# The RWKV core of a decoder step: off-diagonal part of the block inverse written to the other head's rows, outputs in the states' bank, sums of squares behind the betas' product, rows reordered

## The chip, the core and the metric

The kernel runs as one program on one core of one Trainium2 chip. The metric is the device time of one execution in microseconds (us). The engines are named as the profile names them: PE (TensorE), DVE (VectorE), ACT (ScalarE), POOL (GpSimd) and SP (SyncE, which issues the transfers). Every engine works through its own list of instructions in order and waits on semaphores for the others.

## The reference, cut to what matters

The reference is one inference step of a two-layer decoder over 512 prompt tokens and 8 sequences of 8 new tokens: layer 0 mixes with latent attention, layer 1 with RWKV-7 time mixing, and each layer has two SwiGLU feed-forward blocks. The change touches only the state recurrence of layer 1:

```python
def wkv_step(state, inp):
    r, w, k, v, a, b = inp
    sa = jnp.einsum('bhij,bhj->bhi', state, a)
    state = state * w[:, :, None, :] + sa[..., None] * b[:, :, None, :] + v[..., None] * k[:, :, None, :]
    return state, jnp.einsum('bhij,bhj->bhi', state, r)
...
    # in rwkv_time_mix: 16 heads of size 64, a = -kk, b = kk * sigmoid(...), w = decay
    state, y = lax.scan(wkv_step, wkv0.astype(f32), (...))
    mean = jnp.mean(y, axis=-1, keepdims=True)
    var = jnp.mean(jnp.square(y - mean), axis=-1, keepdims=True)
    y = ((y - mean) * lax.rsqrt(var + LNX_EPS)).reshape(b, l, d) * lnx_w.astype(f32) + lnx_b.astype(f32)
    y = y + bonus.reshape(b, l, d)
    out = (y * g.astype(f32)).astype(h.dtype) @ w_o
```

## The kernel before

Most of the program is large matrix products for the feed-forward blocks, the projections and the attention (lines 264 to 2360). The recurrence is a stage of its own, the functions core_pe, core_act, core_dve and core_pool: about 300 us of the span, from roughly 2200 to 2500 us.

The 16 heads are handled two at a time, one head in partitions 0 to 63 and the other in partitions 64 to 127 (HEADS). The 512 prompt tokens are cut into 8 chunks of 64 (NB = 8). Inside a chunk the recurrence becomes a few 64x64 matrices: an inverse of a unit triangular matrix is built by doubling (tiles MD, LD, L2, L4 and XA for the diagonal blocks, then OFF, NT, NR, N2T, N2R, N4R and PP for the part off the diagonal), and a short chain over chunks carries the state (function state(c): a product on PE into the states' bank 4, then a scaled copy to STC on ACT).

The loop is a pipeline of two stages, iteration(f, b). Its front half prepares unit f (unit 0 holds the 64 new tokens, units 1 to 8 are the eight pairs of heads in the prompt), its back half applies unit b = f - 1: states, outputs, their mean and variance, and the gate. So there are nine iterations and a final(8), and eight pairs of heads go through the back half. There is no scheduler: the order on each engine is the order in which these functions are written, and each hand-over is one wait on a named semaphore.

On PE nearly all products are 64x64 with 64 columns. A group is 16 of them (8 chunks, 2 heads); the trace shows two records for each. PSUM is eight banks of 128x512. A product takes its weights and data from the rows of one head and writes either the same head's rows of a bank or, with across=True, the other head's rows. The code often interleaves a group of the one sort with a group of the other, chunk by chunk, into different banks.

The names in the order in which one iteration passes them on PE:

- joint (L2594): products with the new sequences' states S0, 64x16; L2629: PP times RA into RA_PS, the finished R0 and AXT; head_sums(3) for the bonus; AXT times BTOKP (bank 2); R0 times BTOKP (the betas' product, L2545 PS<-R,BTOKP) into the states' bank.
- BT times AR0, then the tiles MD, LD and the doubling; state(1) to state(7) stand between them; gates(f) (L2580) gives the gate of unit f, three products 128x512.
- XA times OFF and back (semaphore z), interleaved with the output's products from MK1 and MB1 (bank 7, L2545); the state's part of the output QQ times STC (bank 7); keys(f+1); NR times NT and NT times NR (semaphore x), the first interleaved with MK0 times the values (bank 6).
- head_sums(5) over the output (its mean), N2R times PP, N2T times N2R, rates(f+1), then XA times RA (L2829, 64x64 with 128 columns, RA_PS in the same head's rows) interleaved with KTOKP times the values, N4R times PP, and head_sums(5) over the squares of the output.

POOL makes, per iteration, PT3 (sums_without_own), YL, the gate product RT (L3417), KKA (rated_keys), BT, K2 and KTI in that order at the turn of two iterations; KTI is what the products KTI and MD, LD at L2587 wait for. DVE adds into PP and XA, takes reciprocals in quarters (L3180, L3195) and has the running sum L3215. ACT copies banks to SBUF and loads a new function table whenever sigmoid, exp and square root follow each other.

Of the kernel before, what the change touches and what calls it, by code (L numbers as in the profile page):

```python
# [28 lines left out]
KD = D // P  # L29
# [69 lines left out]
def program(nc, a, o):  # L99
# [2430 lines left out]
    def core_pe(pe):  # L2530
# [46 lines left out]
        def gates(u):  # L2577
            for out, cols, p in places(u):
                for n, (w, x) in enumerate(((W2H, G1H), (W2H, G1L), (W2L, G1H))):
                    mm = pe.matmul(bank(2)[:, out], w[:, 1, p, :], x[:, cols], start=n == 0, stop=n == 2)  # L2580
            mm.then_inc(q["zag_g"], 1)
# [8 lines left out]
        def joint(p, states):  # L2590

            for j in states:
                for r in HEADS:
                    mm = pe.matmul(bank(0, r)[:, 2 * SQ * j:2 * SQ * (j + 1)].rearrange("p (k q) -> p k q", k=2), S0[r, j, :],  # L2594
                                   AXQ[r, :, p, j * SQ:(j + 1) * SQ], start=True, stop=True)
            return mm

        def iteration(f, b):
# [21 lines left out]
            if chain:  # L2620
# [3 lines left out]
                joint(p, range(0, 3))  # L2624
                wait("rac", b)
                wait("xa", xa_of(b, 4))
                for c in range(NB):
                    for r, out in zip(HEADS, HEADS[::-1]):
                        mm = pe.matmul(RA_PS[out, c], PP[r, c, :], RA[r, c], start=True, stop=True)  # L2629
                    if c < SB - 3:  # L2630
                        x = joint(p, (c + 3,))
                x.then_inc(q["ut"], 1)
# [7 lines left out]
            if chain:  # L2640
# [5 lines left out]
                mm.then_inc(q["gam"], 1)  # L2646
                wait("utc", b)
# [106 lines left out]
            if front:  # L2754
                gates(f)
            state(7)
# [3 lines left out]
            if prompt:  # L2760
                wait("xa", xa_of(f, 2))
            for c in range(NB):
                if prompt:
                    x = products(1, at(OFF), at(XA), (c,))
                if chain:
                    sums(7, at(vtok_b), at(mk1), c, start=True)
            if prompt:
                x.then_inc(q["z"], 1)
            for c in range(NB):
                if prompt:  # L2770
                    x = products(0, at(XA), at(OFF), (c,))
                if chain:
                    mm = sums(7, at(R0), at(mb1), c, start=False)
            if prompt:
                x.then_inc(q["z"], 1)
            if chain:
                mm.then_inc(q["y"], 1)
# [6 lines left out]
                mm.then_inc(q["ys"], 1)  # L2784
            if prompt and f + 1 < UNITS:
# [1031 lines left out]
```

## Time and profile before

| what | value |
|---|---|
| time, median of 3 runs | 2972.98 us (2968.17 to 2975.7) |
| time of the profiled execution | 2976.81 us |
| its span | 2974.6 us |
| PE busy | 2861.9 us, 96% |
| DVE busy | 2100.7 us, 71% |
| ACT busy | 1348.7 us, 45% |
| POOL busy | 698.3 us, 23% |
| chain that ended last, by engine | PE 86%, DVE 7%, ACT 3%, issue 3%, POOL 1% |

Busy time is the sum of an engine's instructions over the whole program; the chain is followed back from the last instruction and says on whom the end depended. In the 200 us slice from 2200 to 2400 us, which lies wholly in the recurrence, PE is busy 179.5 us, DVE 146.6, ACT 128.6 and POOL 107.8, at a granted TensorE clock of 0.98 of full speed. A row of a timeline has the start, the duration, the engine, the line, what is written from what, the shape and the count of merged instructions; in square brackets stands how long the engine sat idle before it and who ended that. "issue" there means that the profile shows nothing it waited for.

### The profile page before, as it was taken

The numbers are of one execution on the slowest core, as the hardware profiler recorded it, in microseconds if no ns is written. First come the engines' busy times: TensorE is split into PE (matmuls) and PEld (weight loads), VectorE is DVE, ScalarE is ACT, GpSimd is POOL, SyncE is SP. The second block draws the span as 40 slices with busy tenths as digits, with TensorE's granted clock in tenths as the row PEclk, the third lists the DMA queues.
The fourth block names the chain that finished last, engine by engine and source line by source line (L and its number), as shares of the span: only waits on it lengthen the run. The fifth ranks groups of instructions, "written<-read, shape, count | busy, mean of one in ns | idle before, by whom it ended". The sixth has DMA issues, their size and how long they took to land.

```text
span 2974.6 us, 65943 instructions
## 1 busy us (share of the span) xinstructions
PE 2861.9 (96%) x27215; PEld 2741.8 (92%) x27215; DVE 2100.7 (71%) x2719; ACT 1348.7 (45%) x2410; POOL 698.3 (23%) x537
## 2 busy tenths in 40 slices
PE   8999999989999998999999999999998997999999
PEld 8999998679999998999999999999987776999999
DVE  6977956656666664697795878775456777487875
ACT  4433434455555552443443344342456664334432
POOL 1321310320000001132131213344034553221330
PEclk9999999999999999999999999999999998999999
DMA  3223222010111121122222232221200001223222
GB/s 121 96 89 99 89 74 81 22 54 26 48 36 37 37 65 57 50 96 96 85 92 86 79 100 89 91 91 58 95 28 15 23 19 56 79 79 100 89 90 81
DMA packets 78970, 208.08 MB, mean 70 GB/s; under 512 B 25505, under 2 KB 42274, under 8 KB 63714
## 3 DMA queue, kind: packets, MB, share of 16 engines
q1 hardware_dynamic: 78690, 204.16, 20.8%
q8 instruction: 199, 3.26, 0.4%
q14 instruction: 81, 0.66, 0.1%
HBM read 198.63 MB, written 5.49 MB: 69 GB/s over the span
## 4 chain that ended last, share of the span: by engine, by line
PE 86%; DVE 7%; ACT 3%; issue 3%; POOL 1%; DMA 0%; POOLq 0%; ACTq 0%; DVEq 0%; SPq 0%
PE PS L469 26%; PE PS L285 23%; PE PS L1595 12%; PE PS L2207 5%; PE PS L642 5%; PE PS L2539 4%; PE PS L1622 1%; PE PS L1574 1%; PE PS L2545 1%; PE PS L2187 1%; DVE WL L269 1%; DVE DOWN L771 1%; DVE WL L435 1%; PE PS L1233 1%; PE PS L1214 1%
## 5 line engine op out<-in xcount | busy, mean ns | idle before, releaser
L408 POOL TENSOR_TENSOR WLF<-RAW 128x512 f32<-128x512 f32 x72 | 94.1, 1307 | 981.2 <-PE PS L285 657.3
L264 ACT ACTIVATE WH<-RAW 128x1536 fp32r<-128x1536 f32 (+3 forms) x112 | 171.4, 1530 | 323.9 <-PE PS L285 195.2
L269 DVE TENSOR_TENSOR WL<-RAW,WH 128x1536 fp32r<-128x1536 f32 (+3 forms) x113 | 217.7, 1927 | 117.8 <-ACT WH L264 117.8
L1595 PE MATMUL PS<-UKMH,CTH 128*128 128x384 f32 (+1 forms) x768 | 269.1, 350 | 0.9 <-POOL RQL L1536 0.9
L469 PE MATMUL PS<-XH,WH 128*128 128x288 f32 x864 | 255.1, 295 | 8.3 <-DVE M L510 8.3
L1671 DVE TENSOR_REDUCE SS<-SQ 128x4 f32<-128x512 f32 x256 | 173.5, 685 | 120.6 <-ACT SQ L1654 118.9
L469 PE MATMUL PS<-XH,WL 128*128 128x288 f32 x864 | 255.5, 296 | 0.0
L469 PE MATMUL PS<-XL,WH 128*128 128x288 f32 x864 | 254.8, 295 | 0.0
L1595 PE MATMUL PS<-UKMH,CTL 128*128 128x384 f32 (+1 forms) x768 | 252.7, 329 | 0.0
L1654 ACT ACTIVATE SQ<-PS 128x384 f32<-128x384 f32 (+1 forms) x384 | 172.3, 455 | 130.3 <-PE PS L1595 130.1
L285 PE MATMUL PS<-HH,WH 128*128 128x288 f32 x1056 | 225.3, 295 | 1.1 <-DVE WL L269 1.1
L285 PE MATMUL PS<-HH,WL 128*128 128x288 f32 x1056 | 226.0, 294 | 0.0
L285 PE MATMUL PS<-HL,WH 128*128 128x288 f32 x1056 | 224.4, 293 | 0.0
L285 PE MATMUL PS<-XH,WH 128*128 128x288 f32 x800 | 174.4, 300 | 18.4 <-DVE XL L308 17.0
L771 DVE TENSOR_TENSOR DOWN<-PS,HALF 128x1152 f32<-128x1152 f32 x64 | 86.7, 1355 | 147.0 <-PE PS L285 104.4
L420 ACT ACTIVATE WH<-RAW 128x1024 fp32r<-128x1024 f32 (+1 forms) x144 | 113.8, 838 | 135.3 <-PE PS L469 76.6
L285 PE MATMUL PS<-XL,WH 128*128 128x288 f32 x800 | 172.5, 298 | 0.0
L285 PE MATMUL PS<-XH,WL 128*128 128x288 f32 x800 | 172.3, 297 | 0.0
L285 PEld LDWEIGHTS PS<-HH,WH 128*128 128x128 f32 x1056 | 169.7, 187 | 2.1 <-DVE WL L269 2.0
L469 PE MATMUL PS<-XSL,WSH 128*128 128x288 f32 x576 | 171.4, 298 | 0.0
L469 PEld LDWEIGHTS PS<-XH,WH 128*128 128x128 f32 x864 | 162.5, 188 | 9.1 <-issue 9.1
L469 PE MATMUL PS<-XSH,WSH 128*128 128x288 f32 x576 | 170.7, 296 | 0.0
(704 smaller groups left out, 8959.4 us busy)
## 6 DMA issues: line engine op xcount, KB each, us to landing
RAW<-in_w SPq DMA_DIRECT2D x113, 1024.0 KB, 4.8
RAW<-in_w SPq DMA_DIRECT2D x48, 768.0 KB, 5.0
ROWS<-in_cache_c SPq DMA_DIRECT2D x128, 128.0 KB, 2.0
RAW<-in_w SPq DMA_DIRECT2D x16, 512.0 KB, 4.6
KRS<-in_cache_kr SPq DMA_DIRECT2D x128, 32.0 KB, 1.8
RAW<-in_w SPq DMA_DIRECT2D x8, 384.0 KB, 3.3
X<-in_x SPq DMA_DIRECT2D x4, 576.0 KB, 8.1
out_y<-X SPq DMA_DIRECT2D x8, 288.0 KB, 2.3
```

Source lines behind the costliest of these rows:

```text
L264: act.activation(WH[n % 2][:, 0:cols], RAW[n % 2][:, 0:cols], ACT.Copy).then_inc(rounded, 1)
L269: dve.tensor_tensor(WL[n % 2][:, 0:cols], RAW[n % 2][:, 0:cols], WH[n % 2][:, 0:cols].bitcast(F32), ALU.subtract).then_inc(item_split, 1)
L285: mm = pe.matmul(PS[:, s, 2 * t + half, 0:HT], w[s][:, c:c + P], v[:, k, half * HT:(half + 1) * HT], start=(x == 0 and p == 0), stop=(x == ...
L420: act.activation(WH[s][:, c], RAW[s][:, c], ACT.Copy).then_inc(gate_hi, 1)
L469: mm = pe.matmul(PS[:, s, b, 0:HT], w[wp](k), v[xp](k), start=not again and k == 0 and p == 0, stop=k == 3 and p == 2, skip_group_check=again)
L642: mm = pe.matmul(PS[:, s, 2 * t + half, 0:HT], w[s][:, c:c + P], v[:, k, half * HT:(half + 1) * HT], start=k == 0 and p == 0, stop=k == cn ...
L771: dve.tensor_tensor(DOWN[:].rearrange("p o (a t) -> p o a t", a=2), ps, halves(HALF[:]).unsqueeze(1).to_broadcast([P, 2, 2, HT]), ALU.mult ...
L1595: mm = pe.matmul(out[:, 0:c1 - c0], c[u][:, x], w, start=t == 0, stop=t == 5)
L1654: act.activation(SQ2[:, at:at + cols], src[:, first:first + cols], ACT.Square).then_inc(keys_sq, 1)
L1671: dve.tensor_reduce(SS[s % 2][:, p, half * 4:half * 4 + 4], SQ2[:, half * 512:half * 512 + 512].rearrange("p (h d) -> p h d", h=4), AX.X, ...
L2207: mm = pe.matmul(PS[:, s, 2 * t + half, 0:HT], w[s][:, c:c + P], v[:, k, half * HT:(half + 1) * HT], start=first and q_ == 0, stop=last an ...
L2539: mm = pe.matmul(cells(b)[out, c, :], lhs(r, c), rhs(r, c), start=True, stop=True)
```

## The change

On PE the products XA times RA (the part of R0 and AXT off the diagonal) are written to the other head's rows of RA_PS, so they can be interleaved with N2R times PP and N2T times N2R; PP times RA now goes to the same head's rows, and the products of joint stand ahead of it. The output is summed in bank 4, the states' bank, after the last state has been copied: the part from the states first, interleaved with MK0 times the values, then the parts from MK1 and MB1, interleaved with NR times NT and NT times NR. The products of XA with OFF lose their partners. gates(f) moves behind NT times NR and, for units above 0, to bank 5. The sums of squares move from the end of an iteration to behind the betas' product of the next. On ACT, DVE and POOL the rows are put in another order. No product is added or dropped.

The diff, cut to its core:

```diff
-                    mm = pe.matmul(bank(2)[:, out], w[:, 1, p, :], x[:, cols], start=n == 0, stop=n == 2)
+                    mm = pe.matmul(bank(5 if u else 2)[:, out], w[:, 1, p, :], x[:, cols], start=n == 0, stop=n == 2)
...
+        def crossed(c):
+
+            for r, out in zip(HEADS, HEADS[::-1]):
+                mm = pe.matmul(RA_PS[out, c], XA[r, c, :], RA[r, c], start=True, stop=True)
+            return mm
+
+        def queried(c):
+
+            for r in HEADS:
+                mm = pe.matmul(cells(4)[r, c, :], STC[r, c - 1, :], QQ[r, c, :], start=c == 1, stop=False, skip_group_check=True)
             return mm
...
                 for c in range(NB):
-                    for r, out in zip(HEADS, HEADS[::-1]):
-                        mm = pe.matmul(RA_PS[out, c], PP[r, c, :], RA[r, c], start=True, stop=True)
-                    if c < SB - 3:
-                        x = joint(p, (c + 3,))
-                x.then_inc(q["ut"], 1)
+                    for r in HEADS:
+                        mm = pe.matmul(RA_PS[r, c], PP[r, c, :], RA[r, c], start=True, stop=True)
                 mm.then_inc(q["r0"], 1)
...
                 mm.then_inc(q["gam"], 1)
+                if p:
+                    wait("y_norm", y_at(p, "sq_lo"))
+                    head_sums(5, YH, YL).then_inc(q["y_norm"], 1)
                 wait("utc", b)
...
+            for c in range(NB):
+                if front:
+                    x = products(6, at(MK0), at(vtok), (c,), across=prompt)
+                if chain and c:
+                    mm = queried(c)
...
+                if chain:
+                    sums(4, at(vtok_b), at(mk1), c, start=False)
...
                     x = products(1, at(NT), at(NR), (c,))
+                if chain:
+                    mm = sums(4, at(R0), at(mb1), c, start=False)
...
+            if prompt:
+                gates(f)
+                wait("pp", f)
+                wait("zc", 3 * f - 1)
+                wait("rvc", n)
+                for c in range(NB):
+                    x = products(2, at(N2R), at(PP), (c,))
+                    if c % 2:
+                        crossed(c // 2)
+                x.then_inc(q["x"], 1)
+                wait("xt", 2 * f)
+                for c in range(NB):
+                    x = products(0, at(N2T), at(N2R), (c,))
+                    if c % 2:
+                        mm = crossed((NB + c) // 2)
...
-                for c in range(NB):
-                    for r in HEADS:
-                        mm = pe.matmul(RA_PS[r, c], XA[r, c, :], RA[r, c], start=True, stop=True)
+                    x = products(2, at(N4RS[f // KD]), at(PP), (c,))
                     sums(4, at(KTOKP), at(vtok), c, start=True)
...
         def decays(u):
+            if u > 1:
+                wait("prev", u + 1)
+                act.activation(flat(E3), flat(PT3), ACT.Exp, scale=DECAY).then_inc(q["e3"], 1)
             wait("cum", u + 1)
...
-            if chain and p:
-                deviation_root(p)
...
                 act.activation(STC[:, 0, :], cells(4)[:, 0, :], ACT.Copy, scale=pcl[:, 0:1]).then_inc(q["stc"], 1)
+                if p:
+                    deviation_root(p)
...
+            if prompt and f + 1 < UNITS:
+                rate_sigmoid(f + 1)
+            if prompt:
+                wait("ra", f)
+                act.activation(RA[:], RA_PS, ACT.Copy).then_inc(q["rac"], 1)
+            if prompt and f + 1 < UNITS:
+                beta_sigmoid(f + 1)
...
             if more:
-                inverse_root(f + 1, range(2, 4))
-                running_sums(f + 1)
-            if chain and p:
-                shifted(p)
+                inverse_root(f + 1, range(2, 3))
             if prompt:
                 wait("x", x_of(f, 5))
                 plus(PP, 2, "xa", xa_of(f, 4))
             if more:
+                running_sums(f + 1)
+                inverse_root(f + 1, range(3, 4))
                 direction(f + 1)
+            if chain and p:
+                shifted(p)
...
+            if more:
+                sums_without_own(f + 1)
             if chain:
                 wait("y_norm", y_at(b, "sq"))
                 pool.tensor_tensor(flat(YL), flat(Y3), flat(YH).bitcast(F32), ALU.subtract).then_inc(q["y_norm"], 1)
             if more:
-                sums_without_own(f + 1)
+                rated_keys(f + 1)
+                scaled_betas(f + 1)
             if chain and p:
                 gate(p)
```

What the change moves, at the three places where the order on an engine matters most. A row has the line, the operation, what is written from what, the shape and the count. The first is PE from the last products NR, NT of an iteration on, before (lines of the kernel before):

```order
L2539 MATMUL PS<-NR,NT 64x64 x16
L2556 MATMUL PS<-YH,BLKR 128x512
L2557 MATMUL PS<-YL,BLKR 128x512
L2539 MATMUL PS<-PP,N2R 64x64 x16
L2539 MATMUL PS<-N2R,N2T 64x64 x16
L2574 MATMUL PS<-THH,WH_55 128x512 x2
L2574 MATMUL PS<-THL,WH_55 128x512 x2
L2574 MATMUL PS<-THH,WL_56 128x512 x2
L2829 MATMUL PS<-RA,XA 64x128 x2
L2545 MATMUL PS<-VTOKB,KTOKP 64x64 x2
L2829 MATMUL PS<-RA,XA 64x128 x2
```

and the same stretch in the changed kernel, from gates(f) on (lines of the changed kernel, where crossed is L2593):

```order
L2580 MATMUL PS<-G1H,WH_55 128x512
L2580 MATMUL PS<-G1L,WH_55 128x512
L2580 MATMUL PS<-G1H,WL_56 128x512
L2539 MATMUL PS<-PP,N2R 64x64 x4
L2593 MATMUL PS<-RA,XA 64x128 x2
L2539 MATMUL PS<-PP,N2R 64x64 x4
L2593 MATMUL PS<-RA,XA 64x128 x2
L2539 MATMUL PS<-PP,N2R 64x64 x4
L2593 MATMUL PS<-RA,XA 64x128 x2
L2539 MATMUL PS<-PP,N2R 64x64 x4
L2593 MATMUL PS<-RA,XA 64x128 x2
L2539 MATMUL PS<-N2R,N2T 64x64 x4
```

The products RA,XA have moved from the partners VTOK,KTOKP to the two groups of the inverse, N2R with PP and N2T with N2R; VTOK,KTOKP now stands beside PP,N4R.

The second is DVE at the turn of two iterations, before (PT_214 is the running sum, KKN the direction, the Y1 row is shifted, AXT and R the copies of RA_PS):

```order
L3229 TENSOR_TENSOR PP<-PP,PS 128x512
L3180 RECIPROCAL RKK<-RKK 128x128 x2
L3215 SCALAR_TENSOR_TENSOR PT_214<-RC,PT_212 128x512
L3210 SCALAR_TENSOR_TENSOR Y1A<-Y1A,VEC,HT__165 128x512
L3229 TENSOR_TENSOR PP<-PP,PS 128x512
L3188 SCALAR_TENSOR_TENSOR KKN<-KT,VEC,RKK 128x512
L3234 COPY AXT<-PS 128x512
L3235 COPY R_209<-PS 128x512
```

and in the changed kernel:

```order
L3217 RECIPROCAL RKK<-RKK 128x128
L3266 TENSOR_TENSOR PP<-PP,PS 128x512
L3252 SCALAR_TENSOR_TENSOR PT_214<-RC,PT_212 128x512
L3217 RECIPROCAL RKK<-RKK 128x128
L3225 SCALAR_TENSOR_TENSOR KKN<-KT,VEC,RKK 128x512
L3247 SCALAR_TENSOR_TENSOR Y1A<-Y1A,VEC,HT__165 128x512
L3271 COPY AXT<-PS 128x512
L3272 COPY R_209<-PS 128x512
```

Running sum, last quarter of the reciprocals, direction and shifted now all stand between the last addition into PP and the copy of AXT, where only the direction stood.

The third is POOL at the same turn, before (PT_216 is sums_without_own, RT the gate product):

```order
L3479 TENSOR_TENSOR PP<-NT,CONST 128x512
L3482 TENSOR_TENSOR YL<-Y_256,YH 128x512
L3421 TENSOR_TENSOR PT_216<-PT_214,PT_212 128x512
L3417 TENSOR_TENSOR RT<-Y1A,KT 128x512
L3426 TENSOR_TENSOR KKA<-KKN,SQA 128x512
L3438 TENSOR_TENSOR BT<-KKA,SQT__226 128x512
L3440 TENSOR_TENSOR K_224<-K_224,KT 128x512
L3446 TENSOR_TENSOR KTI<-K_224,SQT__226 128x512
```

and in the changed kernel:

```order
L3521 TENSOR_TENSOR PP<-NT,CONST 128x512
L3459 TENSOR_TENSOR PT_216<-PT_214,PT_212 128x512
L3526 TENSOR_TENSOR YL<-Y_256,YH 128x512
L3464 TENSOR_TENSOR KKA<-KKN,SQA 128x512
L3469 TENSOR_TENSOR BT<-KKA,SQT__226 128x512
L3455 TENSOR_TENSOR RT<-Y1A,KT 128x512
L3482 TENSOR_TENSOR K_224<-K_224,KT 128x512
L3488 TENSOR_TENSOR KTI<-K_224,SQT__226 128x512
```

YL has moved behind PT_216, and the gate product from ahead of KKA to between BT and K_224.

## Rows read from the trace of the kernel before

**Rows 1.** PE at L2545, R,BTOKP: count, durations in ns, first and last start in us.

```profile
L2545 PE MATMUL PS<-R,BTOKP x256: 218/218/218, 2249.9 to 2489.4; 64*64 64x64 f32 x128
```

**Rows 2.** PE waits, 2240 to 2500 us: who waited, for whom, total, times, longest.

```profile
PE PS L2539 <- issue: 9.8, 18, 1.3
PE PS L2545 <- issue: 5.9, 7, 1.8
PE PS L2539 <- ACT UTS L3019: 3.4, 6, 0.6
```

**Rows 3.** Timeline of PE, 2341 to 2356 us: start, duration, line, operation, count.

```profile
2341.01 0.47 PE L2556 MATMUL PS<-YH,BLKR 128*128 128x512 f32 x1 [0.20 <-DVE YL L3318]
...
2345.08 0.33 PE L2829 MATMUL PS<-RA,XA 64*64 64x128 f32 x2
...
2346.88 1.10 PE L2539 MATMUL PS<-PP,N4R 64*64 64x64 f32 x32
...
2347.91 0.51 PE L2556 MATMUL PS<-YH,BLKR 128*128 128x512 f32 x1
...
2348.57 0.47 PE L2594 MATMUL PS<-AXQ,S 64*64 64x16 f32 x10
...
2350.75 0.50 PE L2556 MATMUL PS<-BOH,BLKR 128*128 128x512 f32 x1
...
2351.61 0.56 PE L2539 MATMUL PS<-BTOKP,AXT 64*64 64x64 f32 x12
...
2354.28 0.27 PE L2539 MATMUL PS<-AIA,BT 64*64 64x64 f32 x2 [0.59 <-ACT UTS L3019]
...
2355.26 0.28 PE L2545 MATMUL PS<-STC,GM 64*64 64x64 f32 x4
```

**Rows 4.** Timeline of PE, 2357 to 2375 us.

```profile
2357.89 0.27 PE L2539 MATMUL PS<-MD,LD 64*64 64x64 f32 x2
...
2365.96 0.50 PE L2580 MATMUL PS<-G1H,WH 128*128 128x512 f32 x1
...
2370.77 0.68 PE L2545 MATMUL PS<-QQ,STC 64*64 64x64 f32 x16
...
2374.31 0.47 PE L2556 MATMUL PS<-YH,BLKR 128*128 128x512 f32 x1 [0.22 <-DVE YL L3318]
```

**Rows 5.** Timeline of DVE, 2341 to 2354 us.

```profile
2341.38 0.94 DVE L3180 RECIPROCAL RKK<-RKK 128x128 f32<-128x128 f32 x1
...
2345.91 1.23 DVE L3215 TENSOR_TENSOR_SCAN PT<-RC,PT 128x512 f32<-128x512 f32 x1
...
2347.05 0.73 DVE L3210 SCALAR_TENSOR_TENSOR Y1A<-Y1A,VEC,HT__165 128x512 f32<-128x512 f32 x1
...
2348.75 0.75 DVE L3188 SCALAR_TENSOR_TENSOR KKN<-KT,VEC,RKK 128x512 f32<-128x512 f32 x1
...
2350.86 0.69 DVE L3234 COPY AXT<-PS 128x512 f32<-128x512 f32 x1 [1.36 <-PE PS L2629]
```

**Rows 6.** Timeline of POOL, 2347 to 2357 us.

```profile
2347.22 1.70 POOL L3421 TENSOR_TENSOR PT<-PT,PT 128x512 f32<-128x512 f32 x1 [1.35 <-DVE PT L3215]
2348.89 1.75 POOL L3417 TENSOR_TENSOR RT<-Y1A,KT 128x512 f32<-128x512 f32 x1
...
2351.95 1.27 POOL L3438 TENSOR_TENSOR BT<-KKA,SQT__226 128x512 f32<-128x512 f32 x1
2353.18 1.73 POOL L3440 TENSOR_TENSOR K<-K,KT 128x512 f32<-128x512 f32 x1
2354.98 1.28 POOL L3446 TENSOR_TENSOR KTI<-K,SQT__226 128x512 f32<-128x512 f32 x1
```

**Rows 7.** POOL at L3421: count, shortest, median and longest in ns.

```profile
L3421 POOL TENSOR_TENSOR PT<-PT,PT x9: 1272/1700/1706, 2188.4 to 2449.5; 128x512 f32<-128x512 f32 x9
```

**Rows 8.** Timeline of ACT, 2341 to 2349 us.

```profile
2341.96 1.28 ACT L3088 ACT_TABLE_LOAD   x1
...
2347.09 1.02 ACT L3100 ACTIVATE RA<-PS 128x1024 f32<-128x1024 f32 x1 [0.63 <-PE PS L2829]
```

## What the change would do: the prediction

> **What bounds the kernel now.** I read the table first: PE is busy 96% and the chain that ended last is 86% PE, so what PE does counts unless another engine makes it wait. The change is confined to the recurrence. There I read the row of the betas' product, which occurs once per pair of heads: eight groups from 2249.9 to 2489.4 us [rows 1]. The last group lasts about 1.0, so seven rounds take 238.6 us, 34.1 us each. Then the waits of PE over these rounds [rows 2]: 3.4 us on the copy UTS of ACT, six times (nearly 0.6 a round), and 15.7 us of "issue", which no engine explains, some 2.1 a round. So PE is close to the bound, and the others run just ahead of it. Last I went through one round row by row, in two stretches. I count u from the end of the products NR, NT; the next row starts at 2341.01 after 0.20 idle [rows 3], so u = 0 is 2340.81. The first stretch runs to the first product MD, LD at 2357.89 (u = 17.08), the second from there to the same end in the next round, 2374.31 less 0.22 = 2374.09 (16.20 us) [rows 4]. This round has 33.3 us; the others have more issue time.
>
> **What PE is spared.** A group of 16 products 64x64 alone takes 2347.91 - 2346.88 = 1.03 us [rows 3]. Two groups that go to different halves of the rows and are interleaved, 30 products, take 2355.26 - 2354.28 = 0.98 [rows 3]: the second costs nothing. XA times RA, with 128 columns, takes 2346.88 - 2345.08 = 1.80 [rows 3] with its partner.
> Second stretch. The states' part of the output now lies beside MK0 times the values, which lost its place beside NR, NT; 14 products at the lone pace, 14/16 x 1.03 = 0.90, go. The parts from MK1 and MB1 change partners and stay hidden. gates(f) leaves; a 128x512 product costs (2348.57 - 2347.91)/2 = 0.33 [rows 3], three cost 1.0 (their first row is at 2365.96 [rows 4]). Together -1.9. The wait for the copy NR is still covered by keys (0.66) and MK0 (1.0).
> First stretch. Out goes 1.80, because the two halves of XA times RA lie beside N2R, PP and N2T, N2R, and KTOKP beside PP, N4R; in come gates, 1.0; joint, interleaved before (2350.75 - 2348.57 = 2.18 with PP times RA [rows 3]), now precedes, +0.1 to 0.3, I take 0.2. The sums of squares, 0.66, only move. Together -0.6; and the UTS wait of 0.59 and the YL wait of 0.20 may go, -0.8. PE alone would allow -1.9 - 0.6 - 0.8 = -3.3 a round.
>
> **What is late next.** I walk the first stretch of a full round again, in u.
> ACT copies N2R, then YH (now behind the end of the output), then the gate, each about 0.5 (half of the 1.02 of a 1024-wide copy [rows 8]); YL on DVE and the copy Y1 follow. The table load of 1.28, which stood at u = 1.15 (2341.96 [rows 8]), starts at about 2.65, and the copy N4R ends at 4.6. PE has done gates, the two groups, the mean and rates (0.9) at 4.55; so PP times N4R runs from 4.65 to 5.65. RA's copy is over at 6.2, PP times RA runs from 6.4 to 8.3, the bonus to 9.0.
> DVE: behind PP, N4R stand the addition into PP (0.65, as the copy AXT is 0.69), the running sum (2347.05 - 2345.91 = 1.14), a reciprocal (0.86 of 0.94, it overlaps), the direction 0.75 and shifted 0.7 [rows 5]; only the first and the direction stood there, and DVE then idled 1.36 ahead of AXT [rows 5]. The running sum ends at 7.5 (before: 2347.05, u = 6.3), AXT begins at 9.8 and is ready at 10.45. PE, done at 9.0, waits 1.5 us. The products from AXT then run to 11.5, the betas' product to 12.5, the squares to 13.2: BT times AR0 starts at 13.2, against 13.47 (2354.28 [rows 3]). ACT needs the UTS copy at 12.0 only, since the square root and its load now stand behind it; that wait is gone.
> POOL: from the running sum, 7.5, follow PT3 1.70, YL 1.27, KKA 1.3, BT 1.27, the gate product 1.75, K2 1.73, KTI 1.28 [rows 6]: 10.3 us in a row, 17.8. BT is ready at 13.1, just in time. KTI was ready at 2356.26, u = 15.45, with 1.6 us to spare; now it is what MD, LD wait for: 17.85 against 17.08, +0.8. The unknown is how long the POOL rows are beside more DVE work: the same PT3 took 1272 to 1706 ns [rows 7]. Three of the seven are at the long end in my sum; all short makes the chain 9.0 and KTI 16.5, below PE's own 16.8; two more long ones add 0.9.
> The short and the long value of one operation in rows 7 say that something blocks it at times. By the Trainium skill (SBUF — State Buffer, section "SBUF: two separate sides") VectorE instructions with two SBUF inputs and GpSimd take one port pair exclusively and the loser waits for the whole instruction; by that rule direction and shifted, which now coincide with this chain, would each cost POOL up to their length, and the walk would end near 18.7 instead of 17.85. The trace agrees as far as 1.27 and 1.70 go. This rule is one ground of rival 3.
> Later in the round AR1 on POOL comes some 0.2 late for XA, L2; with that the first stretch is +1.0, the second -1.9: -0.9 a round.
>
> **The sum.** Five rounds (f = 3 to 7) have the gate product: 5 x -0.9 = -4.5. In f = 2 there is none, KTI comes at 16.1 and PE's own 16.8 holds: -1.9 - 0.2 = -2.1. In f = 8 nothing is prepared for a next unit, so the POOL chain is absent: -1.9 - 0.6 - 0.3 = -2.8, of which the final part gives back 1.0, because ACT's square root with its 1.28 load now stands ahead of the second state copy there: -1.8. In f = 1 only XA, RA is hidden: at most -1.0, I take -0.5. Sum: -8.9. From the profiled execution's 2976.81 that is 2967.9; this execution was 3.8 above the median of the runs, so by the median 2972.98 - 8.9 = 2964.
> Bounds of the unknowns: joint +0.1 to +0.3 a round; N4R's copy hidden or 0.5 later; the POOL chain -1.3 to +0.9; issue time 2.1 a round now, which can be absorbed in the new waits (down to 1) or grow when the stretch gets denser (to 4).
>
> **Rivals.**
> 1. PE stays the bound. POOL's operations stay short and the issue time falls into the new waits: -3.3 + 0.2 for seven rounds, and -1 for the first: -22 at most; with AXT's wait left at half, -20: 2953. For it: 1272 ns in rows 7. Against it: the median there is 1700. 0.20.
> 2. Issue time eats it. Of the 34.1 us a round 2.1 are issue, the longest piece 1.8 [rows 2]; if PE's instructions come too slowly where products are short and interleaved, then gates and the lone states' part, long for their number of instructions, gave time to catch up, and it is they that leave the second stretch. If 1.3 a round come back: 7 x 1.3 = +9, 2973, no change. The Trainium skill (Runtime: NRT & Kernel Launch, "Instruction fetch mechanics") says that the fetch is hidden by the pace of issue, which would give this rival no cause; the trace has the idle time but does not name its source. 0.20.
> 3. Slower: the POOL chain in front of KTI. Place: running sum, seven POOL operations, wait for KTI at the first product KTI (L2587). It decides from KTI at u = 17.08 + 1.9 - 0.2 = 18.8 on. Two more long operations (+0.9), a running sum 0.5 later because N4R waits for the table load, and AR1 late by as much give 19.6: +0.8 a round for six rounds, and nothing from the rest: 2978. For it: seven operations at their short price are already 9.0 us, and the running sum they follow is 1.2 later than before. 0.13.
> 4. The new pairs don't overlap. Then XA, RA stays alone at 1.8 beside the two groups; it comes before the running sum, so half of it, 0.9, reaches the chain behind it, and the other half falls into the wait for N4R's copy and RA's: -8.9 + 7 x 0.9 = -3, 2970. Against it: every interleaved pair of the trace overlaps. 0.05.
>
> **How the numbers follow.** The forecast, -8.9, has 0.42; the others as given. Within 0.3% of the time, 8.9 us, a measurement of this kernel cannot tell a change from none. My forecast lies on that edge: half of its 0.42 is faster. Faster: 0.21 + 0.20 + 0.02 = 0.43. Same: 0.21 + 0.20 + 0.05 - 0.02 = 0.44. Slower: 0.13. The range from 2951 to 2977 holds rival 1 but its extreme, the forecast with its own bounds (2958 to 2970) and nearly all of rival 2 and half of rival 3.
>
> **What would show it.** In the changed profile: rounds of about 33.2 us instead of 34.1 by the betas' product; L2593 beside N2R, PP and N2T, N2R with two groups per 1.0 us; no wait on UTS; instead PE waits on DVE's AXT (about 1.5 a round) and on POOL's KTI (about 0.8); PE busy some 18 us less. I am wrong if PE waits for neither (rival 1), if issue time exceeds 25 us (rival 2), if the wait for KTI exceeds 2 us a round (rival 3), or if the groups with crossed take 1.9 us (rival 4).

## The result, and the profile after

The changed kernel takes 2989.4 us (median of 5 runs, 2982.73 to 2993.57) against 2971.2 us in the same comparison (2967.86 to 2975.7): ratio 1.0052, 95% interval 1.004 to 1.0065. By the ratio it is slower by 0.5%, some 15 us (the two medians are 18.2 apart); forecast were 2964. The profiled execution took 2993.57 us with a span of 2990.7 (before 2974.6).

The loss lies in the recurrence. The betas' product, which [rows 1] showed from 2249.9 to 2489.4, now reads

```profile
L2545 PE MATMUL PS<-R,BTOKP x256: 218/219/312, 2252.1 to 2505.2; 64*64 64x64 f32 x128
```

so seven rounds take 252.1 us (less 1.0 for the last group), 36.0 each instead of 34.1, and in all 13.5 more. The third of the three numbers is the longest product in ns: 218 before, 312 now. The waits of PE, 2240 to 2500 us, that answer to [rows 2] (engine, tile, line, whom it waited for; us in total, times, longest):

```profile
PE PS L2539 <- DVE AXT L3271: 15.8, 7, 2.7
PE PS L2545 <- issue: 6.4, 5, 1.7
PE PS L2539 <- issue: 5.2, 10, 1.3
PE PS L2593 <- issue: 1.8, 4, 0.7
PE PS L2580 <- issue: 1.6, 1, 1.6
```

The wait for UTS is gone, as forecast, and issue time did not grow (15.0 against 15.7 in [rows 2], where 1.5 more stood at L2781). There is no wait for KTI. There is one large new wait, for AXT: 15.8 us in seven rounds, 2.26 each, where 1.5 was forecast.

That is not all of it. The stretches of 20 us with the granted clock as share of full speed (window, its length, PE busy, count, clock, DMA); in the kernel before all of them from 2240 to 2480 show 1.00:

```profile
2320.00:2340.00 20.00, 14.90 (x466) 0.91 0.01 2
2360.00:2380.00 20.00, 18.15 (x598) 0.91 0.01 4
2420.00:2440.00 20.00, 17.17 (x476) 0.83 0.01 3
2460.00:2480.00 20.00, 17.09 (x484) 0.83 0.02 4
```

and in stretches of 2 us around the wait at 2430:

```profile
2426.00:2428.00 2.00, 1.30 (x14) 1.00 0.00 0
2428.00:2430.00 2.00, 0.00 (x0) 0.78 0.00 0
2430.00:2432.00 2.00, 1.97 (x36) 0.50 0.04 8
2432.00:2434.00 2.00, 2.00 (x35) 0.50 0.00 0
2434.00:2436.00 2.00, 2.00 (x46) 0.51 0.00 0
2436.00:2438.00 2.00, 2.00 (x120) 1.00 0.03 8
```

While PE sits idle for 2.73 us its clock falls to the lower of its two levels, 1.2 GHz instead of 2.4, and the next 3 to 6 us run at half speed. The same group of 32 products with AXT in two rounds of this execution (start, duration, ..., idle before and who ended it):

```profile
2396.41 1.15 PE L2539 MATMUL PS<-BTOKP,AXT 64*64 64x64 f32 x32 [2.73 <-DVE AXT L3271]
...
2430.03 1.97 PE L2539 MATMUL PS<-BTOKP,AXT 64*64 64x64 f32 x32 [2.73 <-DVE AXT L3271]
```

Five rounds have that wait of 2.7; four of them are followed by half clock, the one at 2396 is not. This is how one sees it: PE is fully busy there and no wait is named, only the clock column and the longer records tell.

Starts of the groups on PE in the six rounds from one MD, LD to the next, as means in us, give the place of each change (P2 is NR, NT; N4 is N4R, PP; RAPP is RA, PP; BON the bonus; G the products with AXT; BT is BT times AR0). e1 to e13 are the experiments below (there is no e8; e4, e6, e7 and e12 are left out here):

| kernel | MD to P2 | P2 to N2R | N2R to N4 | N4 to RAPP | RAPP to BON | BON to G | G to BT | BT to MD | round |
|---|---|---|---|---|---|---|---|---|---|
| before | 15.55 | 2.07 | 5.16 | 2.04 | 1.89 | 0.86 | 2.65 | 3.84 | 34.05 |
| after | 14.72 | 2.27 | 4.20 | 2.03 | 1.89 | 3.18 | 3.95 | 4.07 | 36.31 |
| e1 | 14.91 | 2.29 | 4.10 | 4.04 | 2.94 | 0.99 | 2.73 | 3.86 | 35.84 |
| e2 | 15.36 | 2.12 | 4.94 | 1.98 | 1.90 | 2.33 | 3.75 | 3.91 | 36.29 |
| e3 | 14.88 | 2.83 | 4.39 | 2.09 | 1.89 | 3.25 | 2.80 | 4.00 | 36.14 |
| e5 | 14.85 | 2.27 | 4.16 | 2.06 | 1.89 | 1.77 | 3.50 | 4.09 | 34.60 |
| e9 | 15.76 | 1.96 | 5.08 | 2.43 | 1.89 | 0.86 | 2.26 | 4.18 | 34.42 |
| e10 | 15.02 | 2.28 | 4.31 | 2.03 | 1.90 | 1.77 | 3.51 | 3.85 | 34.67 |
| e11 | 14.86 | 2.29 | 4.31 | 2.03 | 1.89 | 2.33 | 4.32 | 3.88 | 35.90 |
| e13 | 15.10 | 2.21 | 4.35 | 2.03 | 1.89 | 1.77 | 2.48 | 4.97 | 34.81 |

What PE was to be spared did arrive in part (MD to P2 -0.83, N2R to N4 -0.96). It is lost twice over from the bonus to BT: +2.32 of waiting for AXT, +1.30 behind it. In the round at 2396, at full clock, G to BT takes 2.68; in the four at half clock 3.90, 4.08, 4.77 and 4.76, together 6.8 us more. In the first of the six, 3.51, PE waits for BT.

Why AXT is late shows on DVE from 2422 to 2431 us, the row that answers to [rows 5]:

```profile
2423.84 0.69 DVE L3266 TENSOR_TENSOR PP<-PP,PS 128x512 f32<-128x512 f32 x1 [0.33 <-PE PS L2539]
2424.56 1.22 DVE L3252 TENSOR_TENSOR_SCAN PT<-RC,PT 128x512 f32<-128x512 f32 x1
2425.70 0.93 DVE L3217 RECIPROCAL RKK<-RKK 128x128 f32<-128x128 f32 x1
2426.66 1.02 DVE L3225 SCALAR_TENSOR_TENSOR KKN<-KT,VEC,RKK 128x512 f32<-128x512 f32 x1
2427.61 1.77 DVE L3247 SCALAR_TENSOR_TENSOR Y1A<-Y1A,VEC,HT__165 128x512 f32<-128x512 f32 x1
2429.30 0.68 DVE L3271 COPY AXT<-PS 128x512 f32<-128x512 f32 x1
```

and on POOL beside it, against [rows 6]:

```profile
2425.86 1.27 POOL L3459 TENSOR_TENSOR PT<-PT,PT 128x512 f32<-128x512 f32 x1 [10.78 <-DVE PT L3252]
2427.10 1.73 POOL L3526 TENSOR_TENSOR YL<-Y,YH 128x512 fp32r<-128x512 f32 x1
2428.77 1.73 POOL L3464 TENSOR_TENSOR KKA<-KKN,SQA 128x512 f32<-128x512 f32 x1
2430.58 1.72 POOL L3469 TENSOR_TENSOR BT<-KKA,SQT__226 128x512 f32<-128x512 f32 x1
...
2434.85 1.27 POOL L3488 TENSOR_TENSOR KTI<-K,SQT__226 128x512 f32<-128x512 f32 x1
```

shifted (L3247) takes 1.77 us instead of 0.73 [rows 5], the direction 1.02 instead of 0.75, both under an operation of POOL. Everything ahead of AXT is one unbroken row, and PE waits to its end. KTI ends at 2436.12; PE asks for it at 2438.92.

### The profile page after: what moved, and what is told of

It reads as the page before. It is cut to its first block, busy times and chain, and to the rows that moved or that the text cites. A ratio compares the mean times of both kernels' runs of the same rounds, so it can differ in the third digit from the quotient of the medians.

```text
span 2990.7 us, 65929 instructions
## 1 busy us (share of the span) xinstructions
PE 2868.0 (96%) x27215; PEld 2746.1 (92%) x27215; DVE 2105.6 (70%) x2719; ACT 1346.2 (45%) x2410; POOL 697.9 (23%) x537
## 4 chain that ended last, share of the span: by engine, by line
PE 87%; DVE 7%; issue 3%; ACT 2%; POOL 1%; DMA 0%; POOLq 0%; ACTq 0%; DVEq 0%; SPq 0%
PE PS L469 26%; PE PS L285 23%; PE PS L1595 12%; PE PS L2207 5%; PE PS L642 5%; PE PS L2539 4%; PE PS L1622 1%; PE PS L1574 1%; PE PS L2545 1%; PE PS L2187 1%; DVE WL L269 1%; DVE DOWN L771 1%; PE PS L1214 1%; DVE WL L435 1%; PE PS L1215 1%
```

## The experiments

Each is compared with the kernel before, measured beside it on the same chip (its medians there were 2973.6 to 2975.2); in brackets the 95% interval of the ratio. A difference between two variants is taken from their ratios; by the intervals it is uncertain by some 4 to 6 us. Nothing is left out of the computation in any of them.

**Order on DVE alone.** e1 is the changed kernel with the end of DVE's iteration in the old order; e2 is the kernel before with only this in the new one.

```diff
             if more:
-                inverse_root(f + 1, range(2, 3))
+                inverse_root(f + 1, range(2, 4))
+                running_sums(f + 1)
+            if chain and p:
+                shifted(p)
             if prompt:
                 wait("x", x_of(f, 5))
                 plus(PP, 2, "xa", xa_of(f, 4))
             if more:
-                running_sums(f + 1)
-                inverse_root(f + 1, range(3, 4))
                 direction(f + 1)
-            if chain and p:
-                shifted(p)
```

> The changed kernel with the end of DVE's iteration in the old order: both last quarters of the reciprocals, the running sum and shifted ahead of the last addition into PP, the direction alone behind it. Theory A (DVE queue): the changed kernel waits 15.8 us for the copy AXT in seven rounds because four DVE rows stand ahead of it, and TensorE then falls to half its clock for some us in five of the rounds. Here the AXT wait falls below 3 us and the granted clock stays at 1.00 up to 2480 us; PP times RA starts about 1 us later a round instead, so 10 to 20 us are gained on the changed kernel: 2968 to 2978 against 2971 for the kernel before. Theory B (PE's new rows and banks are slower by themselves): at most 3 us are gained, 2985. Theory C (issue time): no wait for AXT, but issue time grows and the total stays at 2985.

> The kernel before with nothing changed but the end of DVE's iteration, which takes the new order (running sum, last quarter, direction and shifted behind the last addition into PP). Theory A: PE, done with the bonus at u = 10.6, has to wait for AXT some 1.5 to 2.5 us a round and loses clock in some rounds: 10 to 25 us slower than before, 2981 to 2996. Theory B: DVE's order matters little, since PE is the bound in the kernel before: within 5 us of 2971.

Measured: e1 2982.0, 1.0025 (1.0013 to 1.0038), 8 us better than after; e2 2990.8, 1.0060 (1.0043 to 1.0077). The first row is e1's, the other two are e2's waits:

```profile
PE PS L2637 <- DVE PP L3266: 12.7, 7, 2.1
```

```profile
PE PS L2539 <- DVE AXT L3234: 10.6, 7, 1.7
PE PS L2539 <- issue: 15.4, 19, 1.7
```

So DVE's order alone, put into the old kernel, costs as much as the whole change. It does not do so in the same way: from 2240 to 2480 us only one stretch of 20 us in e2 is below full clock (0.91), and the second loss, G to BT +1.10, is a wait for BT. POOL's gate product waits for shifted and KKA and BT stand behind it; in one round BT ends at 2395.47 and PE starts on it at 2395.57, after 1.73 us that the profile names "issue" (the same misnaming as in e5 below). But in the changed kernel the old order is not right either: the AXT wait goes and one for the addition into PP comes, 12.7, since PE reaches that point earlier and DVE has scan, reciprocal and shifted ahead of it. The clock fell in e1 too (0.91 or 0.92 in four stretches of 20 us from 2300 to 2480). The two orders trade one wait for the other; DVE's row as a whole seems too long for PE's new front; that is read from the rows, not tested by itself.

**PE alone.** e4 has PE of the changed kernel and the old orders on DVE, POOL (YL ahead of PT3 again) and ACT; only the square root on ACT stays where its sums now need it.

> The changed kernel with the old order of rows on DVE, on POOL (YL ahead of PT3, gate product ahead of KKA) and on ACT (squares ahead of the copy N4R, both sigmoids ahead of the copy of RA, SQT ahead of E3); only the banks, rows and order of PE are the changed ones, and the square root stays where its sums need it. Theory A (the cost is in DVE's and POOL's order, PE's change is good by 1 us a round): about the time of the run with DVE's old tail or 5 us less, 2972 to 2982. Theory B (PE's new order is what costs): 2985 or more. If ACT's old order is the worse one for the new PE rows, as the change intends, it is slower than the run with only DVE's old tail (2982).

Measured: 2998.0, 1.0082 (1.0066 to 1.0097), the slowest of all by its median. Waits:

```profile
PE PS L2539 <- ACT N4R L3126: 9.9, 6, 1.7
...
PE PS L2637 <- DVE PP L3260: 4.9, 5, 1.2
```

The new orders on ACT and POOL are thus needed by the new PE rows: against e1, which has them, e4 loses 17 us, mostly at N4R's copy (N2R to N4 takes 5.92 a round, 4.10 in e1).

**Filling the wait.** e3 is the changed kernel with six more products 128x512 of PE between the bonus and the wait for AXT; they write bank 2, which the products from AXT then overwrite, so that PE does more work and the output is the same.

```diff
             if chain:
+                for _ in range(3):
+                    head_sums(2, BOH, BOL)
                 wait("axtc", p + 1)
```

> The changed kernel with six more products 128x512 a round (three more times the bonus sums, 2.0 us, into bank 2, which the next group overwrites), put where PE waits for AXT; the output is unchanged. PE works through its wait and nothing on another engine moves. Theory A1 (half of the loss is the clock after the wait): the granted clock stays at 1.00 in the recurrence, the rounds shrink, and it is 5 to 12 us faster than the changed kernel, although PE does 14 us more: 2977 to 2984. Theory A2 (the wait alone costs, the clock does not): the same time as the changed kernel or up to 3 us more, 2987 to 2992.

Measured: 2983.8, 1.0029 (1.0018 to 1.0039): 14 us more work on PE, and about 7 us less time than the changed kernel (the intervals of the two ratios, 1.0018 to 1.0039 and 1.0040 to 1.0065, just fail to meet). The clock shows 1.00 from 2300 to 2500 but for 0.98 and 0.94 in two stretches; G to BT falls from 3.95 to 2.80, while BON to G stays (3.18 and 3.25), as it must if DVE sets the moment. This separates the clock from the wait: G to BT is 1.15 shorter a round though no other engine was touched, 6.9 us in six rounds, as much as the half clock was found to cost above.

**Shifted out of the row.** e5 moves shifted behind the addition GM of the next iteration, and POOL's gate product behind the sums' low part BOL; e6 moves the direction behind the copy of R0 as well.

```diff
                 dve.tensor_tensor(GM[:], cells(2), eye, ALU.add).then_inc(q["gc"], 1)
+                if p > 1:
+                    shifted(p - 1)
...
-            if chain and p:
-                shifted(p)
...
+            if chain and p > 1:
+                gate(p - 1)
...
-            if chain and p:
-                gate(p)
```

> The changed kernel with shifted moved on DVE behind the copy GM of the next iteration and the gate product of POOL moved behind BOL; all the rest in the new order. Theory A: shifted lasted 1.77 us beside POOL and stood in front of AXT; without it AXT comes 1.7 us earlier, PE waits 0.5 us a round, no half clock: 2965 to 2973. KTI also comes 1.3 us earlier. Theory B: 2985.

> The kernel with shifted and the gate product moved back (as in the run before), and in addition the direction moved on DVE behind the copies AXT and R. Theory A: the rest of the wait for AXT, 7.3 us in seven rounds (1.1 a round), goes; the groups after it start 1.1 us earlier unless the betas' operand BT, which needs the direction on POOL, is late in turn. 2968 to 2974 where the kernel before has 2975. Rival: BT, two POOL operations of 1.3 us behind the direction, takes the place of AXT; then PE waits on POOL for most of the 1.1 us and the time is that of the run before, 2977.

Measured: e5 2977.2, 1.0012 (1.0003 to 1.0022), 12 us better than after; e6 2984.4, 1.0032 (1.0021 to 1.0042). e5's waits and e6's:

```profile
PE PS L2539 <- issue: 11.7, 20, 1.0
PE PS L2539 <- DVE AXT L3271: 7.3, 7, 1.0
```

```profile
PE PS L2539 <- issue: 16.9, 13, 2.4
...
PE PS L2539 <- POOL BT L3474: 2.4, 1, 2.4
```

With waits of 1.0 all stretches of e5 from 2240 to 2480 show the full clock. In e6 AXT is never waited for, but the direction is late for KKA and BT on POOL, and the wait stands at BT times AR0. Here "issue" is not what it says: in e5

```profile
2388.85 1.61 POOL L3473 TENSOR_TENSOR BT<-KKA,SQT__226 128x512 f32<-128x512 f32 x1
```

```profile
2390.56 0.27 PE L2539 MATMUL PS<-AIA,BT 64*64 64x64 f32 x2 [0.77 <-issue]
```

BT ends at 2390.46 and PE starts 0.1 later: that looks like a wait for POOL, and e13 tests it.

**What the joint products cost.** They had lain between N4 and RA, PP, and half of them beside RA, PP. e9 is the kernel before with only joint put ahead as a block; e7 is e6 with joint interleaved with the products from AXT; e10 is e5 with joint behind the bonus, in the wait for AXT.

```diff
-                joint(p, range(0, 3))
+                x = joint(p, range(SB))
...
-                    if c < SB - 3:
-                        x = joint(p, (c + 3,))
```

> The kernel before with nothing changed but the place of joint: all 16 products ahead of PP times RA instead of interleaved with it. They have 16 columns; in the kernel before they run beside products for the other head's rows. If a lone product of 16 columns takes as long as one of 64 (1.05 us for 16, as the changed kernel's trace shows), PE has 0.85 us more a round, and as PE is the bound here it is 4 to 7 us slower, 2979 to 2982 against 2975. If my price of 0.2 a round was right it is 1.4 us slower, which cannot be told from nothing.

> As the run with the direction later, and the 16 products of joint interleaved with the products of AXT and BTOKP, which go to the other head's rows, instead of alone ahead of PP times RA. Theory A with the joint term: alone they took 1.05 us a round in the changed kernel, where 0.4 was priced; interleaved they cost nothing, so PP times RA starts up to 0.8 us earlier a round (it still waits for the copy of RA and for PP) and 3 to 6 us go: 2964 to 2971. Rival: PP times RA then waits the same time for the copy of RA or the addition into PP, and nothing is gained.

> The kernel with shifted later (e5, ratio 1.0012) with the joint products, 1.05 us a round, moved from ahead of PP times RA to behind the bonus, that is into PE's wait for AXT (1.0 us in each of 7 rounds there). Theory: AXT is set by DVE's row (PP's addition, scan, reciprocal, direction, copy), not by PE, so PP times RA 1.05 earlier does not move it, and PE's wait is filled: AXT wait near 0, round 34.8 -> 33.8, 7 x 1.0 = 7 us less than e5: about 2970, ratio 0.999. Rival: the copy of AXT waits for PP times RA, so that PE and DVE move together and nothing is gained (2977); or the time comes back as issue idles and at UTS (2975).

Measured: e9 2979.1, 1.0015 (1.0006 to 1.0024); e7 2983.7, 1.0027 (1.0015 to 1.0040), no gain on e6; e10 2978.5, 1.0018 (1.0009 to 1.0027), no gain on e5. In e9 joint adds 0.39 a round where 0.85 was expected (N4 to RAPP) and takes the UTS wait away (G to BT -0.39); the 4 us that it is slower lie elsewhere, 0.34 a round between BT and MD and 0.21 before P2, and their cause is open. In the changed kernel joint as a block, 16 products 64x16 in 32 records, is

```profile
2423.62 1.06 PE L2630 MATMUL PS<-AXQ,S 64*64 64x16 f32 x32
2424.67 1.96 PE L2637 MATMUL PS<-RA,PP 64*64 64x128 f32 x32
```

1.05 us from start to start, as long as a lone group of 64x64 (1.03): with a quarter of the columns it costs the same. That agrees with the Trainium skill (TensorEngine Tiling (Array Packing), section "Instruction Overhead"), by which a product of one column takes as long as one of 60. Why then did e10 gain nothing where it filled an idle microsecond? Its waits say so:

```profile
PE PS L2631 <- DVE PP L3266: 6.1, 7, 0.9
```

In the place it left, joint had covered DVE's addition into PP. N4 to RAPP is 2.03 with and without it. The forecast that went on record for e10 missed this.

**Is it POOL that lengthens shifted?** e11 is the changed kernel with POOL alone altered: it waits for shifted before it goes on from PT3, and YL stands behind BT.

```diff
+            if more and chain and p:
+                wait("y_gate", gate_at(p, "yb"))
+            if more:
+                rated_keys(f + 1)
+                scaled_betas(f + 1)
             if chain:
                 wait("y_norm", y_at(b, "sq"))
                 pool.tensor_tensor(flat(YL), flat(Y3), flat(YH).bitcast(F32), ALU.subtract).then_inc(q["y_norm"], 1)
-            if more:
-                rated_keys(f + 1)
-                scaled_betas(f + 1)
```

> The changed kernel with only POOL's row altered: after PT3 it waits for shifted to end, then KKA, BT, and YL behind them. No work is dropped. Theory (POOL's YL and KKA block shifted): shifted falls from 1.77 and 1.43 to 0.73, the AXT wait of the full rounds from 2.7 to about 1.7, and with a shorter idle stretch the clock falls less; KTI comes 0.8 later but still before PE asks. Time 2989 -> about 2980 (5 x 1.0 for the wait, 3 to 4 for the clock). Rival 1: shifted's length is its own (a strided operand), it stays at 1.77 and the time stays at 2989. Rival 2: BT late by 0.9 stops PE at BT times AR0, time as after or worse (2990).

Measured: 2984.6, 1.0042 (1.0029 to 1.0056). Groups of DVE by form, 2240 to 2500 us (count, busy us, mean ns of one, idle before), of the changed kernel, of e2 and of e11:

```profile
L3247 DVE SCALAR_TENSOR_TENSOR Y1B<-Y1B,VEC,HT__165 128x512 f32<-128x512 f32 x3 | 5.3, 1765 | 0.0
L3247 DVE SCALAR_TENSOR_TENSOR Y1A<-Y1A,VEC,HT__165 128x512 f32<-128x512 f32 x3 | 4.3, 1433 | 0.0
```

```profile
L3210 DVE SCALAR_TENSOR_TENSOR Y1A<-Y1A,VEC,HT__165 128x512 f32<-128x512 f32 x3 | 2.2, 742 | 0.0
```

```profile
L3247 DVE SCALAR_TENSOR_TENSOR Y1A<-Y1A,VEC,HT__165 128x512 f32<-128x512 f32 x3 | 3.0, 1011 | 0.0
L3247 DVE SCALAR_TENSOR_TENSOR Y1B<-Y1B,VEC,HT__165 128x512 f32<-128x512 f32 x3 | 2.2, 739 | 0.0
```

In the five full rounds the same instruction in the same place takes 1.76 to 1.78 with POOL at work and 0.74 with POOL held off; in e2, whose POOL is idle at that moment, it is 0.74 too. The two means of Y1A that lie between take in the last iteration, where POOL has another row and is not held off (0.75 there in the changed kernel, 1.56 in e11). The waits of e11 for AXT:

```profile
PE PS L2539 <- DVE AXT L3271: 10.6, 7, 1.7
PE PS L2556 <- POOL YL L3531: 7.8, 5, 1.6
```

2.7 has become 1.7, as expected, and only one stretch of 20 us is still below 0.99 (0.92, at 2360). Part of the gain, 5.2 us of this wait and most of the half clock, went into a wait of 7.8 us for YL, which nobody had named (rival 2 had the right kind of reason, with the wrong tile): G to BT is 4.32. So the whole gained 3 us by the ratios and not the 9 expected, and the two intervals overlap: e11 shows what lengthens shifted, but not that the kernel as a whole is faster by it.

**Behind the betas' product.** e12 is e10 with YL behind BT; e13 is e12 with the squares on PE, and the square root on ACT, moved behind state(1) and UU.

```diff
                 mm.then_inc(q["gam"], 1)
-                if p:
-                    wait("y_norm", y_at(p, "sq_lo"))
-                    head_sums(5, YH, YL).then_inc(q["y_norm"], 1)
...
                 mm.then_inc(q["us"], 1)
+                if p:
+                    wait("y_norm", y_at(p, "sq_lo"))
+                    head_sums(5, YH, YL).then_inc(q["y_norm"], 1)
```

> e10 with YL on POOL behind KKA and BT instead of ahead of them. Theory: in e5 DVE's AIA took 1.65 beside POOL's row and BT came at the time when PE asks for it; with YL later KKA starts as soon as the direction is there, BT 1 us earlier, YL still before the squares. If BT or GM bounds behind the betas' product, 0.3 to 0.5 a round: 2 to 4 us less than e10. Rival: YL is then late for the squares (they follow the betas' product), a wait of some 0.5 a round, 3 us more than e10.

> The kernel before this one (joint in AXT's wait, YL on POOL behind BT: ratio 1.0038 with a wait of up to 2.0 for YL at the squares) with the sums of squares on PE moved on behind BT times AR0, state(1) and the product that gives UU, and ACT's square root with its table load behind the copy UU. No work is dropped. Theory: with shifted out of the way, what stops PE behind the betas' product is POOL's row PT3, YL, KKA, BT (0.77 idle a round ahead of BT times AR0 in the kernel with joint in the wait); with YL behind BT, and the squares where YL has had time, both that idle and the YL wait go: G to BT 3.50 -> 2.1, the squares 0.66 come back later: 0.7 a round, 5 us less than the kernel with joint in the wait, about 2973, ratio 0.9995 to 1.000. Rival: the wait moves once more, to the square root (ATOK's products wait for it, and the copies of the states stand behind it on ACT): 0.5 to 1 a round, 2978 to 2983.

Measured: e12 2985.4, 1.0038 (1.0024 to 1.0052), the rival, with

```profile
PE PS L2556 <- POOL YL L3535: 11.8, 6, 2.0
```

and e13 2976.6, 1.0010 (1.0000 to 1.0019). In e13 the row ahead of BT times AR0 is

```profile
2397.67 0.27 PE L2539 MATMUL PS<-AIA,BT 64*64 64x64 f32 x2 [0.40 <-issue]
```

and POOL's BT ends at 2397.56, 2.37 us after the start of G; in e10 it ended 3.41 after. PE starts 0.1 after it in both, and G to BT falls from 3.51 to 2.48: the "issue" ahead of BT is a wait for POOL's BT, of which 0.40 is left. BT to MD took 1.1 more than in e10, 0.66 of it the squares. e13 has the lowest ratio of the variants, though it cannot be told from e5 (1.0012); by its interval it is between level with the kernel before and 0.2% slower. No version faster than the kernel before was found.

## Why the prediction was wrong

The step that failed is "What is late next", in its DVE row: "AXT begins at 9.8 and is ready at 10.45. PE, done at 9.0, waits 1.5 us." In the round at 2410 to 2450, where u = 0 is 2417.48, the copy begins at u = 11.82 and is ready at 12.5, and PE is done at about 9.8. A second term failed too, the 0.90 us that the states' part of the output was to save; it saved nothing (below). In detail:

- DVE starts the addition into PP at u = 6.36, the walk had it at about 5.7: +0.7, with N4 over later than forecast. Direction and shifted were priced at the lengths of [rows 5], 0.75 and 0.7, and took 1.02 and 1.77: +1.3. These two make the copy 2.0 late. The prediction priced two operations that meet on POOL alone, as a delay of KTI (its 18.7 is 17.85 and two long operations; the two lengths in full would have made 19.3), and in the end KTI never was waited for. Here shifted met POOL's YL already running, and the one that was lengthened stood on PE's path. The Trainium skill (SBUF — State Buffer, section "SBUF: two separate sides") lets either engine be the loser, whichever starts second. The trace agrees with the rule, 0.74 against 1.77 (e11). The trace before had a row of it, just behind those of [rows 5], beside POOL's BT [rows 6]; in the round at 2249 the same instruction took 0.69, and POOL's K beside it 1.72:

```profile
2352.07 1.70 DVE L3239 SCALAR_TENSOR_TENSOR AIA<-KKN,E 128x512 f32<-128x512 f32 x1
```

- The wait grew less than AXT's delay, because PE was 0.8 late as well, 0.57 of it by joint: it is 1.05 as a block, so that with RA, PP it takes 2.95 where the sum had 2.18 + 0.2.
- The clock was not in the sum at all. The longest wait of [rows 2] is 1.8 us, so no row shown before priced one of 2.7; the trace before does have granted clocks of 0.89 and 0.94 in the two stretches from 2200 to 2240, which the prediction did not read. The fall is 6.8 us by the six rounds and about 7 by e3.

Point by point: the second stretch was to give -1.9; MD to P2 gave -0.83. Idle time is not the cause: it is 1.7 us a round in both kernels. The gates (1.0) left as forecast, but the other term, 0.90 for the states' part QQ times STC, was wrong. In the kernel before, MK0 times the values cost nothing beside NR, NT; now it needs the time that QQ times STC had had alone. From the start of this part to NT, NR it was 0.86 in rounds without idle time and is 1.37, 0.22 of it a wait (first two rows before, last two after):

```profile
2303.19 0.97 PE L2545 MATMUL PS<-QQ,STC 64*64 64x64 f32 x26
2304.05 0.22 PE L2539 MATMUL PS<-NT,NR 64*64 64x64 f32 x1
```

```profile
2306.86 0.27 PE L2539 MATMUL PS<-VTOKA,MK 64*64 64x64 f32 x2
2308.23 0.27 PE L2539 MATMUL PS<-NT,NR 64*64 64x64 f32 x2 [0.22 <-PE PS L2599]
```

The new pairs overlap: N2R to the mean with both halves of XA, RA takes 2.06 in one full round, and 2.3 to 2.4 in the others once the idle time ahead of RA, XA (0.13 to 0.73) is taken off, so rival 4 was rightly low. The UTS wait went. The wait for KTI, +0.8 and rival 3, did not come: PE itself was later, and PT3 became shorter where it was priced at 1.70:

```profile
L3459 POOL TENSOR_TENSOR PT<-PT,PT x9: 1270/1273/1382, 2190.7 to 2463.4; 128x512 f32<-128x512 f32 x9
```

Issue time did not grow, against rival 2. PE busy rose by 6 us (2868.0 against 2861.9) where -18 was forecast, because records at half clock are longer; e5, at full clock, has 2853.1, which is -9. A round of the six misses its forecast by 3.2 us (+2.3 against -0.9): 1.1 is the second stretch, and the rest lies in the first, where the AXT wait had the right mechanism at half its size (2.7 against 1.5 in a full round) and the half clock a price that was not in the sum.

What was shown by experiment: DVE's order alone is enough for a loss of this size in the kernel before (e2), and undoing it in the changed one gives back 8 of the 15 us (e1); shifted's length is POOL's work beside it (e11), the half clock costs some 7 us (e3), the row's length and not joint sets AXT (e10), BT is the next bound (e13). Read from rows and not tested: why the gain of the second stretch shrank. Open: why e9 lost 4 us.

## What to carry to other kernels

Before an operation is moved into a row that another engine waits for, look at what POOL does in that moment: its length there is not the length in its old place, and the loser may be the engine on the path. A wait on TensorE can have two prices, its length and the half clock behind it. Its length alone does not tell whether the second is paid. With waits for other engines of up to 1.0 us (e5) none of the twelve stretches of 20 us from 2240 to 2480 was below full clock; with waits of up to 1.7 it was one in e2, two in e11 and six in e4, with 2.0 five (e12), with 2.1 six (e1), with 2.4 three (e6 and e7) and with 2.7 four. So look at the clock column of each variant instead of reckoning from the wait. And an idle gap can be filled at no gain when the filler covered something where it came from.

## What the runs showed of the hardware that was not expected

- PE at 1.2 GHz after 2.73 us of idling, for 3 to 6 us: a group of 32 records went from 1.15 to 1.97 us. It also fell in kernels with no idle time over 2.1 us there (e1, e4).
- A DVE operation with two SBUF inputs went from 0.74 to 1.77 us beside POOL, and POOL's from 1.27 to 1.73.
- Products of 64x16 cost what 64x64 cost when alone: 1.05 us against 1.03 for the group.
- Idle time that the profile names "issue" was, ahead of BT times AR0, a wait for POOL: PE started 0.1 us after BT ended, and 1.03 us earlier when BT ended 1.04 earlier (e13).
